# ScalarE forms the high parts of the next head's weight units in the first layer; GpSimd is left with the low parts

## The reference, cut to what is computed

```python
q, fz, i, g = split(x @ w_in)            # x: 1152 tokens, w_in: 1024 x 4096
q = silu(q);  f = lb + (1 - lb) * sigmoid(fz)
k = 1 - f;    v = i
S_t = diag(f_t) S_{t-1} + k_t v_t^T;     o_t = S_t^T q_t      # per head
o = rms_norm(o) * silu(g)
```

## Time and profile before

| What | Value |
|---|---|
| median of three runs | 3089.18 us (3088.5 to 3097.56) |
| the profiled execution: own time | 3094.78 us |
| the profiled execution: span from first to last instruction | 3092.9 us |
| PE busy | 2995.9 us, 97% of the span |
| DVE busy | 1707.4 us, 55% |
| ACT busy | 690.6 us, 22% |
| POOL busy | 1009.3 us, 33% |
| mean granted TensorE clock | 0.988 of full speed |

### The profile page before, as it was taken

The page is one execution under the profiler, slowest core; times in us unless marked ns, Lnnn a source line. Parts: engine busy times, 40 slices in busy tenths (PEclk is TensorE's granted clock), DMA queues, the critical chain, the costliest instruction groups (busy, mean ns, idle before and its releaser), DMA issues.

```text
span 3092.9 us, 42638 instructions
## 1 busy us (share of the span) xinstructions
PE 2995.9 (97%) x17108; PEld 2780.6 (90%) x17108; DVE 1707.4 (55%) x2425; ACT 690.6 (22%) x1314; POOL 1009.3 (33%) x428
## 2 busy tenths in 40 slices
PE   6999999999999999999999999998999999999998
PEld 6999999987899999999987888887899999999997
DVE  3677777776654444444445565555755444444446
ACT  2333333342111111111123233233111111111112
POOL 3122222222143333333334233215034333333324
PEclk9999999999999999999999999999999999999999
DMA  3111111113111111111112112003111111111102
GB/s 121 43 37 33 42 35 35 41 42 112 38 59 42 41 41 41 41 41 41 49 60 98 37 45 70 27 29 122 40 55 42 48 41 41 41 45 43 41 28 91
DMA packets 193002, 155.82 MB, mean 50 GB/s; under 512 B 10252, under 2 KB 176204, under 8 KB 192844
## 3 DMA queue, kind: packets, MB, share of 16 engines
q1 hardware_dynamic: 192920, 154.64, 16.2%
HBM read 135.34 MB, written 19.28 MB: 50 GB/s over the span
## 4 chain that ended last, share of the span: by engine, by line
PE 89%; DVE 5%; ACT 2%; issue 2%; POOL 1%; DMA 1%; POOLq 0%; SPq 0%; ACTq 0%; DVEq 0%
PE bank L684 26%; PE bank L686 26%; PE bank L685 26%; PE bank L858 5%; PE bank L716 1%; PE bank L771 1%; DVE h_c L1381 1%; PE bank L779 1%; PE bank L786 1%; PE bank L763 1%; DVE stats L1299 1%; PE bank L706 1%; DVE xt_lo L1293 0%; PE bank L823 0%; ACT xt_hi L1031 0%
## 5 line engine op out<-in xcount | busy, mean ns | idle before, releaser
L623 POOL TENSOR_TENSOR ring_hi<-ring_raw,ones 128x1024 fp32r<-128x1024 f32 x197 | 440.6, 2237 | 1957.2 <-DMA ring_raw<-in_ffn_w_up 736.7
L684 PE MATMUL bank<-xt_hi,ring_hi 128*128 128x384 f32 (+1 forms) x2712 | 913.9, 337 | 8.9 <-DVE xt_lo L1287 5.8
L685 PE MATMUL bank<-xt_lo,ring_hi 128*128 128x384 f32 (+1 forms) x2712 | 909.6, 335 | 0.0
L686 PE MATMUL bank<-xt_hi,ring_lo 128*128 128x384 f32 (+1 forms) x2712 | 909.6, 335 | 0.0
L684 PEld LDWEIGHTS bank<-xt_hi,ring_hi 128*128 128x128 f32 (+1 forms) x2712 | 509.4, 188 | 17.4 <-DVE xt_lo L1287 7.1
L685 PEld LDWEIGHTS bank<-xt_lo,ring_hi 128*128 128x128 f32 (+1 forms) x2712 | 509.6, 188 | 4.4 <-issue 1.7
L686 PEld LDWEIGHTS bank<-xt_hi,ring_lo 128*128 128x128 f32 (+1 forms) x2712 | 509.4, 188 | 1.9
L626 POOL TENSOR_TENSOR ring_lo<-ring_raw,ring_hi 128x1024 fp32r<-128x1024 f32 x197 | 504.1, 2559 | 15.5
L684 PE MATMUL bank<-ring_hi,xt_hi 128*128 128x256 f32 (+1 forms) x1152 | 401.3, 348 | 6.4 <-POOL ring_lo L626 6.4
L686 PE MATMUL bank<-ring_hi,xt_lo 128*128 128x256 f32 (+1 forms) x1152 | 391.1, 339 | 0.0
L685 PE MATMUL bank<-ring_lo,xt_hi 128*128 128x256 f32 (+1 forms) x1152 | 390.9, 339 | 0.0
(11 more groups left out here) (176 smaller groups left out, 3158.4 us busy)
## 6 DMA issues: line engine op xcount, KB each, us to landing
ring_raw<-in_ffn_w_up SPq DMA_DIRECT2D x88, 512.0 KB, 3.9
ring_raw<-in_ffn_w_down SPq DMA_DIRECT2D x44, 512.0 KB, 4.0
ring_raw<-in_hgrn_w_in SPq DMA_DIRECT2D x16, 512.0 KB, 5.1
tm<-in_x_prompt SPq DMA_DIRECT2D x16, 512.0 KB, 6.3
ring_raw<-in_hgrn_w_in SPq DMA_DIRECT2D x32, 256.0 KB, 3.7
ring_raw<-in_gla_w_in SPq DMA_DIRECT2D x32, 256.0 KB, 4.5
x_scratch<-tm SPq DMA_DIRECT2D x9, 512.0 KB, 2.6
tm<-x_scratch SPq DMA_DIRECT2D x9, 512.0 KB, 3.4
```

The costliest lines, as they stand in the source:

```text
L623: nc.gpsimd.tensor_tensor(ring_hi[slot][:, 0:width], ring_raw[slot][:, 0:width], ones[:, :].to_broadcast([P, width]), ALU.mult).then_inc(u ...
L684: nc.tensor.matmul(dst, w_hi, x_hi, start=start, stop=False)
L685: nc.tensor.matmul(dst, w_hi, x_lo, start=False, stop=False)
L686: return nc.tensor.matmul(dst, w_lo, x_hi, start=False, stop=stop)
```

## The change

From head 1 on, ScalarE copies each raw unit of layer 0's mixer into `ring_hi` (a copy rounds to fp32r) and signals `head_hi`; POOL waits for that and does only the subtraction (`head_lows`). Head 0's four units stay wholly with POOL. ScalarE makes the copies for slots 0 and 1 of head i+1 inside head i, behind the exponentials of level 2 and ahead of `take_vg(1)`; those for slots 2 and 3 at the start of head i, behind the sigmoid of the gate and ahead of the copies of the transposed keys (`token_keys`). Head 7 is written out behind ScalarE's loop, because it has no next head. The remaining edits (`HI_ACT` in `skipped`) adjust the counts of a semaphore for the 28 high parts that POOL no longer makes.

```diff
+        HI_ACT = 4 * (HEADS_H - 1)
...
-            def split(unit, slot, count, width=UNIT, by_act=0, skipped=0):
-                if by_act:
-                    pool.wait_ge(w_hi, by_act)
+            def split(unit, slot, count, width=UNIT, by_act=0, skipped=0, act_sem=w_hi):
+                if type(by_act) is not int or by_act > 0:
+                    pool.wait_ge(act_sem, by_act)
...
+            def head_lows(i):
+
+                for s in range(4):
+                    split(i * 4 + (U_H + s), s, None, by_act=i * 4 + (s - 3), act_sem=head_hi)
...
-            with pool.Fori(0, HEADS_H) as i:
-                head_units(KIND["h"], i)
+            head_units(KIND["h"], 0)
+            with pool.Fori(1, HEADS_H) as i:
+                head_lows(i)
...
-            def attention(K, i, first, last_):
+            def attention(K, i, first, last_, next_=True):
...
+                def high_parts(j, slots):
+
+                    for s in slots:
+                        act.wait_ge(slot_in[s], slot_count("h", j, s))
+                        activate(ring_hi[s][:, :], ring_raw[s][:, :], ACT.Copy).then_inc(head_hi, 1)
...
                     if not first and not last_:
+                        high_parts(i, (2, 3))
                         token_keys()
...
                 for t in range(NL - 1):
                     level(t + 1)
+                    if t == 1 and n == "h" and next_:
+                        high_parts(i + 1, (0, 1))
                     take_vg(t)
...
-            with act.Fori(1, HEADS_H) as i:
+            with act.Fori(1, HEADS_H - 1) as i:
                 attention(KIND["h"], i, False, False)
+            attention(KIND["h"], HEADS_H - 1, False, False, False)
             attention(KIND["h"], HEADS_H, False, True)
```

More of the change, by code:

```diff
@@ L252, in build @@
         unit_hi = sem("unit_hi")
+        head_hi = sem("head_hi")
         w_hi = sem("w_hi")
@@ L637, in head_units @@
                 for s in range(s0, K["units"]):
-                    split(i * K["units"] + (K["unit0"] + s), s, slot_count(K["n"], i, s), skipped=(0 if K["n"] == "h" else 4))
+                    split(i * K["units"] + (K["unit0"] + s), s, slot_count(K["n"], i, s), skipped=(0 if K["n"] == "h" else HI_ACT + 4))
+            def head_lows(i):
+                for s in range(4):
+                    split(i * 4 + (U_H + s), s, None, by_act=i * 4 + (s - 3), act_sem=head_hi)
             def out_units(layer, base, unit0):
                 for u, slot in enumerate(W_SLOTS):
-                    split(unit0 + u, slot, 16 * (base[slot] + 1), by_act=(4 * layer + u - 3 if u >= 4 else 0), skipped=4 * layer)
+                    split(unit0 + u, slot, 16 * (base[slot] + 1), by_act=(4 * layer + u - 3 if u >= 4 else 0),
+                          skipped=HI_ACT + 4 * layer)
             def ffn_units(base, unit0, skipped):
@@ L658, in ffn_units @@
                     split(unit0 + (6 * GROUPS - 2 + u), slot, 16 * (base[slot] + GROUPS + 1), skipped=skipped)
-            with pool.Fori(0, HEADS_H) as i:
-                head_units(KIND["h"], i)
+            head_units(KIND["h"], 0)
+            with pool.Fori(1, HEADS_H) as i:
+                head_lows(i)
             out_units(0, slot_base["wh"], U_WH)
-            ffn_units(slot_base["f0"], U_F0, 4)
-            split(U_R, R_SLOT, 16 * (slot_base["r"][R_SLOT] + 1), KD * RANK, skipped=4)
-            split(U_G, 0, slot_count("g", 0, 0), skipped=4)
+            ffn_units(slot_base["f0"], U_F0, HI_ACT + 4)
+            split(U_R, R_SLOT, 16 * (slot_base["r"][R_SLOT] + 1), KD * RANK, skipped=HI_ACT + 4)
+            split(U_G, 0, slot_count("g", 0, 0), skipped=HI_ACT + 4)
             add_shift(0)
-            split(U_G + 1, 1, slot_count("g", 0, 1), skipped=4)
+            split(U_G + 1, 1, slot_count("g", 0, 1), skipped=HI_ACT + 4)
             pool.wait_ge(FSIG["down"].sem, DOWN_ALL)
@@ L676, in _ @@
             out_units(1, slot_base["wg"], U_WG)
-            ffn_units(slot_base["f1"], U_F1, 8)
+            ffn_units(slot_base["f1"], U_F1, HI_ACT + 8)
             add_shift(1)
```

## The result

The changed kernel takes 3061.77 us (median of 4 runs, 3060.53 to 3063.89); the kernel before 3090.53 (median of 4, the three earlier runs and one more, 3088.5 to 3097.56). The ratio is 0.9901, 95% interval 0.9888 to 0.9913. That is 28.8 us less by these medians and 27.4 less than the 3089.18 from which the prediction started; 27.2 less, and 3062, were forecast.

The account below looks back on a forecast made before the run. PE bounds the kernel (busy 97%), losing time to VectorE's level 1 multiplies colliding with POOL's split. Gains of 20.0 + 3.7 + 3.5 = 27.2 us take 3089.18 to 3062, range 3053 to 3076.

Parts of the forecast that it names:

- POOL's high parts go: Layer 0's heads: without POOL's 28 high parts, level 1 is ready at 238.6 and PE starts it without a stop.
- ScalarE's copies cost nothing: Copies of 1.06 us each on ScalarE: free in time for level 3 by about 0.1 us; cost nothing.
- the rival in which ScalarE waits for a late load: Level 3's exponentials and PE stand behind late loads; slower past 12 us of slip, 3110 with 15 us; chance 0.05.
- the 8.17 us of cover: ScalarE's idle time before the transposed keys, said to cover 2.1 us of copies for slots 2 and 3 and a late load.
- The low parts move: Slots 0 and 1: low parts begin at about 242, behind level 3's subtraction; a 0.85 us stall stays at level 3.
- the 2.8 that the prediction had named as a sign: Level 3's multiplies were to take 1.5 and 2.8 us beside POOL's low parts.
- the bound of 3.1 us a head: Lower bound of a head's gain, against 4.0 taken, if the score placing must wait for POOL too (one more 0.85).
- The sum: Layer 0's heads: 20.0 for heads 1, 2, 4, 5, 6, plus 3.7 for head 3, 3.5 for head 0: 27.2 us.
- the slow clock, for which 2.6 us had been taken off: Head 0: slow clock likely to stay after PE's waits of 2.6 and about 2 us, so 3.5 taken instead of 6.1.
- The slow clock: Rival: low clock follows the 0.85 us wait at level 3, costing 1.63 us a head; 3073.6; chance 0.2.
- some stall stays: Forecast 0.85 us stall at level 3, against the rival that VectorE wins the turns and none stays: 3054, chance 0.1.
- the collision can move bodily: Rival: low parts hold up level 3 by 1.9 us and the clock falls; gain 9 us, 3080; chance 0.1.

Follow-up runs that it names:

- The single halves: Kernel before with only slots 2 and 3's high parts on ScalarE: 3095.72 us, ratio 1.0011; with only slots 0 and 1's: 3061.92 us, ratio 0.9900.

## Why the prediction was right, point by point

**POOL's high parts go.** Right. Level 1's multiplies are at 0.69 us, PE goes into level 1 of heads 1 to 6 without a wait, and head 2 takes 77.40 us where about 77 was named as a sign. The single halves show that slots 0 and 1 are the whole of it.

**ScalarE's copies cost nothing.** Right: 1.05 us each, idle time behind both pairs, and with the low parts left out they cause no wait. The copies of slots 0 and 1 waited for no DMA, as the prediction said. The copy of slot 3 waited 0.85 us for its load (0.4 to 0.9 us in each of the heads), the only trace of the rival in which ScalarE waits for a late load; the 8.17 us of cover that the prediction named for such a load took it, and 5.51 were left.

**The low parts move.** Right in the result, wrong in the order. The prediction had VectorE's subtraction go ahead of the first low part, because a POOL instruction that comes while VectorE runs end to end had waited for all of it. In the changed kernel the first low part went ahead: it shows from 230.89, during the multiply that ends at 231.19, and the subtraction of 231.11 was held up by 2.2 us; then only the first multiply met the second low part, 1.55 us, while the second was at 0.75 and not at the 2.8 that the prediction had named as a sign. The wait came out at 1.08 us instead of 0.85, because the delays add up to nearly the same either way: 2.2 + 0.8 us found, 0.75 + 2.05 forecast. That the wrong order hardly changed the sum is luck. The score placing of line 1416 ran at 0.78 us for two while the second low part was under way (234.57), so the bound of 3.1 us a head did not apply. This is what the Trainium skill (SBUF - State Buffer, "Who interferes with whom") says of a VectorE instruction with at most one SBUF input, outside the modes in which VectorE takes both ports, and here the trace agrees. That section of the Trainium skill also has issue order decide who blocks, and this is not settled here: by the starts that the profile shows it fits the changed kernel (POOL at 230.89, the subtraction at 231.11) and not the kernel before, where POOL, started at 232.75, waited for the multiply of 233.76 as well.

**The sum.** Heads 1 and 2 gain 3.76 each on average against 4.0, the difference being the longer wait; head 3 gains 3.39 against 3.7, heads 4 to 6 11.15 against 12.0, head 7 nothing, as forecast. Head 0 gains 7.36 - 1.7 = 5.7 against 3.5, the one term clearly mis-sized: its multiplies were freed as forecast and 2.94 and 1.53 us of wait at levels 0 and 1 stayed, but the slow clock, for which 2.6 us had been taken off, did not come. The granted clock from 66 to 86 us, around levels 0 and 1 of head 0, was 1.00 in the changed kernel; before, it was 0.68 and 0.50 there. So 27.2 were forecast and 27.7 found in layer 0's heads, but heads 1 to 6 came 1.6 short and head 0 gave 2.2 more: that the two nearly cancel is luck, and the step behind the 2.2, whether a low clock follows a wait, stays open.

**The rivals.** The slow clock did not stay behind the 1.08 us wait. That some stall stays was right for this place of the copies; two levels later none stayed. That the collision can move bodily was shown, not by the change but by the variant that made POOL wait for the whole split.

## What to carry to other kernels

Where an instruction on the critical chain takes several times its usual duration in one place, look for the engine that is busy just there and compare the ends: a turn-by-turn collision shows as an end that lies about the usual duration behind the other engine's end. Count how many of the other engine's instructions fall between two points where the chain meets the bound engine, and compare that with the slack at that point; move the work to where the slack is largest (here two levels later: a ratio of 0.9861 to the kernel before in place of 0.9901), and not merely away. Taking work off an engine is worth nothing where its instructions hide, as slots 2 and 3 did.

## What the runs showed of the hardware that was not expected

Who goes first when both engines want a turn was not settled, and the starts that the profile shows differ by less than 0.1 us between the two outcomes. In the kernel with slots 2 and 3 alone on ScalarE, POOL's first high part got in ahead of VectorE's subtraction where it started 0.09 to 0.15 us sooner (heads 1, 3 and 6), and behind it and the multiply after it where it started 0.07 us sooner (heads 2 and 5) or 0.05 us later (head 4); the wait of PE was 5.1 or 3.26 us accordingly. In the kernel before, POOL waited for two VectorE instructions in a row (4.11 us); with the wait added, and in the changed kernel, POOL got in between two that ran end to end (the 2.38 us multiply and the 3.54 us subtraction). Starts as the profile gives them do not tell these apart.

The granted clock does not follow from the length of a wait alone: after 3.26 us it fell in five heads before and not in head 3, after 2.17 us it fell in head 7, after 2.62 us in head 7 of the kernel with copies behind level 4 it did not, and after 2.94 and 1.53 us, 2 us apart, it did not fall in head 0 of the changed kernel.
